# The token shift of the first projection: from TensorE matmuls with a shift matrix to DMA copies inside SBUF

## The chip, the cores and the metric

The kernel runs on one core of a Trainium2 chip. The metric is the device time of one execution in microseconds (us). Three executions of the kernel before took 3198.28, 3200.54 and 3200.67 us, so the median is 3200.54 us. A profiled execution, from which every row below is taken, took 3198.18 us.

## The reference, cut to what matters

The whole computation is two transformer-like blocks over 256 tokens of width 2048. The change touches one place, near the start: the input projection of the first block, and the token shift that follows it.

```
u   = x @ w_in                       # 256 x 2048 times 2048 x ...; the first 3360 columns are z
z_prev[0]  = 0
z_prev[t]  = z[t-1]                  # the row of the token before
z   = z + mu * (z_prev - z)          # mu: one value for each of the 3360 columns
r, k, v, zw, za, zg = split(z)       # feeds the rwkv stage: tanh, sigmoid, three small projections, the scan
```

The other columns of `u` (mlstm and gates) are not shifted. They are projected later in the kernel.

## The kernel before, in words

**Layout.** Tokens lie on the 128 partitions in two halves b = 0 and 1, so `UR` is [128 partitions, 2 halves, 3360 columns]: token 128*b + p is row p of half b. The row of the token before is thus one partition up, and for row 0 of half 1 it is row 127 of half 0.

**Stage "in".** The 3360 columns are done in seven chunks, ci = 0 to 6: six of 512 columns and one of 288. For each chunk TensorE multiplies `xT` by eight pieces of `w_in` (`pieces_a`, lines 590 to 620); a piece is 256 rows of the weight by the width of the chunk. All products are done in two halves of precision: a piece gives 12 matmuls (2 halves of tokens, 2 blocks of rows, 3 products of high and low parts), so a chunk has 96. The sum of a chunk is in a PSUM buffer; ScalarE copies it into `UR` (`out_of`, line 2709, event `ur.copied`). TensorE then waits for that copy and multiplies the chunk by two constant matrices, `shiftd` (one above the diagonal, minus one on it) and `carry` (the one row that passes from half 0 to half 1), lines 1282 to 1287: three plain fp32 matmuls over the width of the chunk, which the trace shows as six. They give z_prev - z in PSUM. VectorE multiplies that by mu in place and adds it to `UR` (lines 2246 to 2248, event `ur`). `mub`, the broadcast of mu, lies at `fmbase`.

**The weight pieces.** One stream of pieces serves the whole projection. SyncE loads a piece into one of six raw buffers as soon as the piece six places earlier has been halved (`pieces`, line 2962). ScalarE writes its high part, and VectorE (or GpSimd, for pieces that are marked so) subtracts to get the low part (`split_to`, line 207). There are three pairs of high and low buffers, so piece i can be halved only when TensorE has used piece i - 3. Every engine runs its own program in order; a call `split_to(j)` in an engine's program says at which point it does the pieces before j, and `ahead_of(key)` does those up to two beyond the last piece of that sum. Pieces 0 to 55 are those of the seven chunks, eight each, halved by VectorE. The pieces of the projection `ml.qk`, which follow, are halved by GpSimd.

**PSUM.** Four buffers of 1024 columns (`Ring`, `take`, line 116). TensorE takes the one that was taken longest ago, and waits until whoever reads it has freed it. The shift took a buffer of its own for each chunk.

**Order of the stages around it.** After chunk 6 and its shift, TensorE does three pieces of `ml.qk` (`rwkv`, line 691), then waits for `ur.gates`: tanh and sigmoid by ScalarE on the last columns of the shifted z (line 2375). It transposes them (`rw.lo`), does two more pieces of `ml.qk`, and then needs `ur.loraT`, which VectorE makes (lines 1402 to 1415) behind two products and two sums over the shifted k. GpSimd's program (line 2795) makes constants, issues eight loads for parameters, and then begins to halve the `ml.qk` pieces (`g.ahead_of("ml.qk", 1)`, line 2845).

Of the kernel before, what the change touches and what calls it, by code (L numbers as in the profile page):

```python
# [9 lines left out]
ALU = mybir.AluOpType  # L10
# [328 lines left out]
def build(nc, I, out, plan=None, last=False):  # L339
    with ExitStack() as ctx:  # L340
# [7 lines left out]
        def at(o, n, dt=F32):  # L348
            names[0] += 1
            assert o + n <= TOT, o + n  # L350
            return nc.alloc_sbuf_tensor_at(f"t{names[0]}", [128, n], dt, offset=base + 4 * o)[:, :]

        def alloc(n, dt=F32):
            o = top[0]
            top[0] = o + n + -n % 8
            return at(o, n, dt)

        def tm(c):
            return alloc(2 * c).rearrange("p (b c) -> p b c", b=2)
# [7 lines left out]
        def bufs(nraw, nhalf):  # L367
# [6 lines left out]
        ring = Ring(psum, plan.get("ring", {}))  # L374


        ident, shiftd, carry, ucent, tri_inc, tri_str = [alloc(128) for _ in range(6)]
        invm_at = top[0]
        invm = alloc(7 * 128)
        level = invm[:, 0:384].rearrange("p (l t) -> p l t", l=6)  # L380
# [8 lines left out]
        xT = [blocks[:, :, h, :] for h in range(2)]  # L389
# [3 lines left out]
        UR = tm(3360)  # L393
# [5 lines left out]
        fmbase = top[0]  # L399
# [9 lines left out]
        lt_at = top[0]  # L409
# [5 lines left out]
        kstate = alloc(8 * 64).rearrange("p (i v) -> p i v", i=8)  # L415
        pz = alloc(8)
        mub = at(fmbase, 3360)
        par = [RB.rearrange("p b c -> p (b c)")[:, 0:1024], RB.rearrange("p b c -> p (b c)")[:, 1024:2048],
               at(lt_at + 1280, 1024)]
        r_, k_, v_ = [UR[:, :, 1024 * i:1024 * i + 1024] for i in range(3)]  # L420
# [24 lines left out]
        sm2 = alloc(8 * 16).rearrange("p (k b h) -> p k b h", k=8, b=2)  # L445
        bg = alloc(32)
        gains = [at(invm_at + 768 + 16 * k, 16) for k in range(2)]
        diag = [shiftd, carry]
        assert top[0] <= invm_at + 896
        R = [rw[0:8, k, :] for k in range(8)]  # L450
        vhm = vm.rearrange("p b (h n) -> p b h n", n=128)
# [112 lines left out]
        def two(v, n):  # L564
            return v.unsqueeze(1).broadcast_to([128, 2, n])

        def half(v):
            return v.rearrange("p (b n) -> p b n", b=2)
# [5 lines left out]
        def tensor_program(e):  # L574
            pe = Tensor(e, counts, ring, stream, ident)

            def turn_columns(key, src, j, *after, of=(0, 1, 2, 3)):

                v = pe.take(key, j, of=of).rearrange("p (b k t) -> p b k t", b=2, k=4)
                pe.wait_ge(*after)  # L580
                for b in range(2):
                    for k in range(4):
                        pe.tr(v[:, b, k, :], src[:, b, 512 * j + 128 * k:512 * j + 128 * k + 128],
                              event=(key, j) if b == 1 and k == 3 else None)
# [62 lines left out]
            def proj_a(*args, **kw):  # L647
                for _ in pieces_a(*args, **kw):
                    pass
# [5 lines left out]
            def some(work, n):  # L655
                for _ in range(n):
                    next(work, None)
# [614 lines left out]
            for j, part in enumerate(((0,), (0, 1), (1, 2), (2, 3, 3))):  # L1272
                turn_columns("in.xT", x, j, (f"landed.in{j}",), ("ident",))
                for i in part:
                    pe.wait_ge(("in.xTc", i))
                    some(first, 1)
            pe.wait_ge(("consts",))
            for ci, c in enumerate(range(0, 3360, 512)):
                n = min(512, 3360 - c)
                if ci:  # L1280
                    proj_a(pe, f"ur{ci}", xT, 16, "w_in", c, n)
                v = half(pe.take("ur.shift", ci))[:, :, 0:n]
                d = UR[:, :, 512 * ci:512 * ci + n]
                pe.wait_ge(("ur.copied", ci))
                pe.mm(v[:, 0, :], shiftd, d[:, 0, :], True, True)
                pe.mm(v[:, 1, :], shiftd, d[:, 1, :], True, False)
                pe.mm(v[:, 1, :], carry, d[:, 0, :], False, True, event=("ur.shift", ci))
            pe.stage("rwkv")
            rwkv()
            rows_of("ml.if", "w_if", xT, (0, 8), 8, "pool")  # L1290
# [10 lines left out]
            v = pe.take("pl.T", of=(2,)).rearrange("p (k b t) -> p k b t", k=4, b=2)  # L1301
# [51 lines left out]
        def vector_program(e):  # L1353
            v = Vector(e, counts, ring, stream)
# [878 lines left out]
                    attended(u)  # L2233

            v.stage("in")
            v.stage("in")
            for j in range(4):
                v.split_to(2 * j + 1 if j else 0)
                low_half("in.xT", xT, j, "in.xTc")
                v.split_to(2 * j + 2)  # L2240
            for ci, c in enumerate(range(0, 3360, 512)):
                n = min(512, 3360 - c)
                v.ahead_of("ur.shift", ci)
                ps = half(v.bank("ur.shift", ci))[:, :, 0:n]
                d = UR[:, :, 512 * ci:512 * ci + n]
                v.wait_ge(("ur.shift", ci), ("landed.mu",))
                v.tt(ps, ps, two(mub[:, 512 * ci:512 * ci + n], n), ALU.mult)
                v.tt(d, d, ps, ALU.add, event=("ur", ci))
                v.free("ur.shift", ci)
            v.stage("rwkv")  # L2250
            rwkv()
            gate_rows()
# [13 lines left out]
            for c in range(4):  # L2266
# [8 lines left out]
                     event=("mi.lo", c))  # L2275
# [63 lines left out]
            for ci in range(4):  # L2339
                cs = slice(512 * ci, 512 * ci + 512)  # L2340
                for b in range(2):
                    v.stt(hn[:, b, cs], x[:, b, cs], inv[:, b:b + 1], rwt[:, cs], ALU.mult, ALU.mult,
                          event=("out.h", ci) if b else None)
# [451 lines left out]
        def pool_program(e):  # L2795
            g = Pool(e, counts, ring, stream)
# [2 lines left out]
            g.memset(ones, 1.0)  # L2799
            g.memset(ident, 0.0)  # L2800
            g.asel(ident, ident, ALU.not_equal, 1.0, 0, [[-1, 128]], 1, event=("ident",))
            g.memset(shiftd, 0.0)
            g.asel(shiftd, shiftd, ALU.not_equal, 1.0, 1, [[-1, 128]], 1)
            g.asel(shiftd, shiftd, ALU.not_equal, -1.0, 0, [[-1, 128]], 1)
            g.memset(carry, 0.0)
            g.asel(carry, carry, ALU.not_equal, 1.0, -127, [[128, 128]], 1)
            g.asel(tri_inc, one, ALU.is_ge, 0.0, 0, [[1, 128]], -1)
            g.asel(tri_str, one, ALU.is_gt, 0.0, 0, [[1, 128]], -1)
            g.memset(ucent, -CD)
# [4 lines left out]
            for l in range(6):  # L2814
                b = 1 << l
# [20 lines left out]
            def along(name):  # L2836
                return I[name][0].partition_broadcast(128)
# [3 lines left out]
                                    (gb[0:8, 1:2], I["f_bias"].rearrange("o h -> h o")), (bg, I["b_gate"])])  # L2841
            g.load(("landed.par",), [(par[0], along("k_k")), (par[1], along("k_a")),
                                     (par[2], I["r_k"][0].rearrange("h n -> (h n)").partition_broadcast(128))])
            g.stage("rwkv")
            g.ahead_of("ml.qk", 1)
            for b in range(2):
# [65 lines left out]
            for l in range(5):  # L2912
                n = 1 << l
# [6 lines left out]
            for l in range(3):  # L2920
                n = 1 << l
# [99 lines left out]
        with nc.Block() as block:  # L3021
            @block.sync
            def _(e):
                sync_program(e)

            @block.tensor
            def _(e):
                tensor_program(e)

            @block.vector  # L3030
            def _(e):
                vector_program(e)

            @block.scalar
            def _(e):
                scalar_program(e)

            @block.gpsimd
            def _(e):
                pool_program(e)  # L3040
# [55 lines left out]
```

## Time and profile before

| what | value |
|---|---|
| median of three executions | 3200.54 us |
| the profiled execution's own time | 3198.18 us |
| its span, from first to last instruction | 3196.4 us |
| TensorE busy | 3009.0 us, 94% of the span |
| VectorE busy | 1547.4 us, 48% |
| ScalarE busy | 837.8 us, 26% |
| GpSimd busy | 283.5 us, 9% |
| HBM read | 720.28 MB, 226 GB/s over the span |

In the trace PE is TensorE, DVE is VectorE, ACT is ScalarE, POOL is GpSimd and SP is SyncE; a q behind a name is that engine's sequencer. Code lines are those of the helpers (L137 matmul, L254 activation, L283 tensor_tensor of VectorE, L328 tensor_tensor of GpSimd, L83 a load), so instructions of a stage are found by time. Stage "in" with its shift runs from the start to about 192 us.

### The profile page before, as it was taken

What the parts mean: (1) busy time and instruction counts of PE and PEld (TensorE: products, weight loads), DVE (VectorE), ACT (ScalarE), POOL (GpSimd) and SP (SyncE); (2) the same over time, 40 slices, a digit from 0 to 9 for tenths busy, and PEclk for the clock granted to TensorE, in tenths of its full rate; (3) what the DMA queues carried; (4) which work ended last, traced back from release to release, by engine and by line L of the source; (5) the groups of instructions that cost most, each with busy time, mean ns of one, the idle gap of its engine ahead of it and who ended that gap; (6) DMA issues with size and microseconds to landing.
All of it is one profiled execution on the core that took longest, in us unless ns stands there. A gap on an engine that the chain in (4) does not pass through costs nothing.

```text
span 3196.4 us, 42548 instructions
## 1 busy us (share of the span) xinstructions
PE 3009.0 (94%) x18244; PEld 2161.4 (68%) x18244; DVE 1547.4 (48%) x1846; ACT 837.8 (26%) x926; POOL 283.5 (9%) x260
## 2 busy tenths in 40 slices
PE   8999999899999999999999999879999998999898
PEld 6777777899977743333333333268858878998886
DVE  4465544674556522222222222357887554444765
ACT  3352221544434310110110110010000243444443
POOL 2042111000000000000000000035440000000100
PEclk9999988999998999999999999989999999999999
DMA  7543221446575599999999999843333355898543
GB/s 244 151 139 100 74 61 58 123 140 182 174 237 171 190 366 425 425 425 425 425 425 425 425 425 425 341 159 118 114 124 118 126 178 125 194 194 183 137 165 138
DMA packets 216144, 725.25 MB, mean 227 GB/s; under 512 B 16314, under 2 KB 18794, under 8 KB 165644
## 3 DMA queue, kind: packets, MB, share of 16 engines
q1 hardware_dynamic: 210716, 702.22, 62.6%
q0 software_dynamic: 4144, 18.14, 1.6%
q8 instruction: 145, 2.38, 0.3%
q10 hardware_dynamic: 1088, 2.10, 0.2%
q14 instruction: 51, 0.42, 0.0%
HBM read 720.28 MB, written 2.11 MB: 226 GB/s over the span
## 4 chain that ended last, share of the span: by engine, by line
PE 72%; DMA 12%; DVE 11%; ACT 4%; issue 1%; POOL 0%; DVEq 0%; ACTq 0%
PE psum L137 71%; DMA t<-in_w_up 12%; DVE t L283 8%; ACT t L254 2%; PE psum L143 2%; DVE t L294 1%; ACT t L256 1%; DVE t L298 1%; DVE t L306 0%; ACT L254 0%; POOL t L328 0%; DVE t L269 0%; ACT L256 0%; DMA t<-in_x 0%; DVE t L275 0%
## 5 line engine op out<-in xcount | busy, mean ns | idle before, releaser
L137 PE MATMUL psum<-t,t 128*128 128x256 f32 (+7 forms) x17166 | 2914.8, 379 | 135.3 <-DVE t L283 78.8
L137 PEld LDWEIGHTS psum<-t,t 128*128 128x128 f32 (+4 forms) x17166 | 2069.7, 175 | 941.2 <-issue 564.2
L283 DVE TENSOR_TENSOR t<-t,t 128x1024 fp32r<-128x1024 f32 (+6 forms) x642 | 786.0, 1224 | 495.8 <-ACT t L254 462.5
L254 ACT ACTIVATE t<-t 128x1024 fp32r<-128x1024 f32 (+8 forms) x521 | 528.6, 1015 | 901.4 <-PE psum L137 625.3
L283 DVE TENSOR_TENSOR t<-t,psum 128x1024 f32<-128x1024 f32 (+3 forms) x265 | 246.3, 929 | 741.3 <-PE psum L137 440.7
L254 ACT ACTIVATE t<-psum 128x1024 f32<-128x1024 f32 (+5 forms) x278 | 213.5, 768 | 1414.9 <-PE psum L137 1315.5
L328 POOL TENSOR_TENSOR t<-t,t 128x1024 f32<-128x1024 f32 (+8 forms) x133 | 222.9, 1676 | 571.7 <-DVE t L283 258.2
L283 DVE TENSOR_TENSOR t<-psum,t 128x1024 f32<-128x1024 f32 (+6 forms) x117 | 101.1, 864 | 121.9 <-PE psum L137 91.8
L143 PE MATMUL psum<-t,t 128*128 128x128 f32 (+1 forms) x566 | 87.9, 294 | 31.7 <-DVE t L294 18.0
L143 PEld LDWEIGHTS psum<-t,t 128*128 128x128 f32 (+1 forms) x566 | 67.6, 150 | 69.5 <-issue 39.8
L83 POOL DMA_DIRECT2D t<-in_s_lr x1 | 0.6, 574 | 1187.2 <-DVE t L306 1187.2
L269 DVE COPY t<-psum 128x256 f32<-128x256 f32 (+4 forms) x74 | 44.4, 600 | 106.4 <-PE psum L143 59.7
L294 DVE SCALAR_TENSOR_TENSOR t<-t,t,t 128x512 f32<-128x512 f32 (+4 forms) x80 | 49.4, 618 | 3.0
L254 ACT ACT_TABLE_LOAD x38 | 48.8, 1283 | 4.6 <-issue 1.4
L298 DVE TENSOR_REDUCE t<-t 128x4 f32<-128x512 f32 (+9 forms) x58 | 47.5, 819 | 2.4 <-ACT t L254 0.4
L302 DVE TENSOR_TENSOR_SCAN t<-t,t 128x256 f32<-128x256 f32 (+1 forms) x65 | 44.7, 688 | 2.2
L137 PE MATMUL psum<-t 64*64 64x64 f32 (+2 forms) x512 | 36.3, 269 | 6.6 <-ACT t L254 5.8
L290 DVE TENSOR_SCALAR t<-t,t,t 128x64 f32<-128x64 f32 x128 | 40.2, 314 | 4.6
L137 PEld LDWEIGHTS psum<-t 64*64 64x64 f32 (+2 forms) x512 | 30.1, 174 | 10.1 <-ACT t L254 7.5
L83 POOL DMA_DIRECT2D f_rows<-t x1 | 0.6, 555 | 383.7 <-DVE t L302 383.7
L269 DVE COPY t<-t 64x64 f32<-64x64 f32 x64 | 30.2, 472 | 2.2
L256 ACT ACTIVATE t<-psum,t 128x256 f32<-128x256 f32 (+1 forms) x56 | 24.8, 444 | 21.5 <-PE psum L137 15.1
(67 smaller groups left out, 240.1 us busy)
## 6 DMA issues: line engine op xcount, KB each, us to landing
t<-in_w_gate SPq DMA_DIRECT2D x128, 1024.0 KB, 16.9
t<-in_w_up SPq DMA_DIRECT2D x128, 1024.0 KB, 18.4
t<-in_w_down SPq DMA_DIRECT2D x128, 1024.0 KB, 17.5
t<-in_w_in SPq DMA_DIRECT2D x160, 512.0 KB, 4.1
t<-in_w_in_odd SPq DMA_DIRECT2D x128, 512.0 KB, 5.4
t<-in_w_in_even SPq DMA_DIRECT2D x96, 512.0 KB, 3.8
t<-in_w_out SPq DMA_DIRECT2D x32, 512.0 KB, 4.3
t<-in_w_pg SPq DMA_DIRECT2D x32, 512.0 KB, 4.3
```

Of the source, the lines that this page charges most:

```text
L83: self.e.dma_start(out, in_).then_inc(self.counts.sem(name), 16)
L137: ins = self.e.matmul(o, l, r, start=start, stop=stop, skip_group_check=True)
L143: ins = self.e.transpose(o, i, self.ident[0:k, 0:k])
L254: self.put(self.e.activation(o, i, f, scale=scale), event)
L256: self.put(self.e.activation(o, i, f, bias=bias, scale=scale), event)
L269: self.put(self.e.tensor_copy(o, i), event)
L283: self.put(self.e.tensor_tensor(o, a, b, op), event)
L290: self.put(self.e.tensor_scalar(o, a, s1, s2, o1, o2), event)
L294: self.put(self.e.scalar_tensor_tensor(out=o, in0=a, scalar=s, in1=b, op0=o1, op1=o2), event)
L298: self.put(self.e.tensor_reduce(o, i, AX.X, op), event)
L302: self.put(self.e.tensor_tensor_scan(o, d0, d1, init, o0, o1), event)
L328: self.put(self.e.tensor_tensor(o, a, b, op), event)
```

## The change

The shift matmuls, their PSUM buffers and the two constant matrices go. In their place GpSimd waits for ScalarE's copy of a chunk and issues three DMA copies inside SBUF, which bring `UR` one partition down into a buffer `earlier[ci % 2]`: rows 0 to 111, rows 112 to 126, and the one row that goes from half 0 to half 1. VectorE then does three operations on SBUF (subtract, multiply by mu, add) instead of two. Row 0 of half 0 of the buffer is kept at zero by a memset. VectorE halves the pieces before 8*ci + 12, four pieces into the next chunk, before it waits for the copies of chunk ci. TensorE goes from chunk to chunk without the shift.

```diff
-        ident, shiftd, carry, ucent, tri_inc, tri_str = [alloc(128) for _ in range(6)]
+        ident, diag0, diag1, ucent, tri_inc, tri_str = [alloc(128) for _ in range(6)]
...
+        earlier = [at(o, 1024).rearrange("p (b c) -> p b c", b=2) for o in (fmbase + 3360, lt_at + 2304)]
...
# TensorE
+            for ci in range(1, 7):
+                proj_a(pe, f"ur{ci}", xT, 16, "w_in", 512 * ci, min(512, 3360 - 512 * ci))
             pe.wait_ge(("consts",))
-            for ci, c in enumerate(range(0, 3360, 512)):
-                n = min(512, 3360 - c)
-                if ci:
-                    proj_a(pe, f"ur{ci}", xT, 16, "w_in", c, n)
-                v = half(pe.take("ur.shift", ci))[:, :, 0:n]
-                d = UR[:, :, 512 * ci:512 * ci + n]
-                pe.wait_ge(("ur.copied", ci))
-                pe.mm(v[:, 0, :], shiftd, d[:, 0, :], True, True)
-                pe.mm(v[:, 1, :], shiftd, d[:, 1, :], True, False)
-                pe.mm(v[:, 1, :], carry, d[:, 0, :], False, True, event=("ur.shift", ci))
...
# VectorE
+            for z in earlier:
+                v.mset(z[0:1, 0, :], 0.0, event=("ur.first",))
...
             for ci, c in enumerate(range(0, 3360, 512)):
                 n = min(512, 3360 - c)
-                v.ahead_of("ur.shift", ci)
-                ps = half(v.bank("ur.shift", ci))[:, :, 0:n]
-                d = UR[:, :, 512 * ci:512 * ci + n]
-                v.wait_ge(("ur.shift", ci), ("landed.mu",))
-                v.tt(ps, ps, two(mub[:, 512 * ci:512 * ci + n], n), ALU.mult)
-                v.tt(d, d, ps, ALU.add, event=("ur", ci))
-                v.free("ur.shift", ci)
+                v.split_to(8 * ci + 12)
+                d, z = UR[:, :, c:c + n], earlier[ci % 2][:, :, 0:n]
+                v.wait_ge((f"landed.shift{ci % 2}", ci), ("landed.mu",))
+                v.tt(z, z, d, ALU.subtract)
+                v.tt(z, z, two(mub[:, c:c + n], n), ALU.mult)
+                v.tt(d, d, z, ALU.add, event=("ur", ci))
+                v.mset(z[0:1, 0, :], 0.0)
...
# GpSimd
-            g.memset(shiftd, 0.0)
-            g.asel(shiftd, shiftd, ALU.not_equal, 1.0, 1, [[-1, 128]], 1)
-            g.asel(shiftd, shiftd, ALU.not_equal, -1.0, 0, [[-1, 128]], 1)
-            g.memset(carry, 0.0)
-            g.asel(carry, carry, ALU.not_equal, 1.0, -127, [[128, 128]], 1)
...
+            for ci, c in enumerate(range(0, 3360, 512)):
+                n = min(512, 3360 - c)
+                d, z = UR[:, :, c:c + n], earlier[ci % 2][:, :, 0:n]
+                g.wait_ge(("ur.copied", ci), ("ur", ci - 2) if ci > 1 else ("ur.first",))
+                g.load((f"landed.shift{ci % 2}", ci), [(z[1:113], d[0:112]), (z[113:128], d[112:127]), (z[0:1, 1], d[127:128, 0])])
             g.stage("rwkv")
             g.ahead_of("ml.qk", 1)
```

## Rows read from the trace of the kernel before

**Rows 1.** The page: TensorE's busy time, and the chain that ended last by engine.
```profile
PE 3009.0 (94%) x18244; PEld 2161.4 (68%) x18244; DVE 1547.4 (48%) x1846; ACT 837.8 (26%) x926; POOL 283.5 (9%) x260
...
PE 72%; DMA 12%; DVE 11%; ACT 4%; issue 1%; POOL 0%; DVEq 0%; ACTq 0%
```

**Rows 2.** The chain of waits in order of time: start us, us, what.
```profile
38.88 1.03 ACT t L254
...
40.05 25.12 PE psum L137 x102
65.20 1.03 ACT t L254
...
171.49 2.86 PE psum L137 x6
...
187.67 0.66 ACT t L254
...
199.24 1.06 PE psum L143 x8
200.30 25.70 PE psum L137 x164
```

**Rows 3.** TensorE's timeline: start, us, instruction, count, [idle before <- releaser].
```profile
177.77 9.86 PE L137 MATMUL psum<-t,t 128*128 128x288 f32 x72 [0.25 <-DVE t L283]
188.37 10.36 PE L137 MATMUL psum<-t,t 128*128 128x288 f32 x78 [0.74 <-ACT t L254]
```

**Rows 4.** VectorE's timeline, same columns.
```profile
45.49 2.58 DVE L283 TENSOR_TENSOR t<-t,t 128x1024 fp32r<-128x1024 f32 x2
...
183.64 0.76 DVE L283 TENSOR_TENSOR t<-t,t 128x576 fp32r<-128x576 f32 x1 [0.84 <-ACT t L254]
...
191.79 3.53 DVE L283 TENSOR_TENSOR t<-t,t 128x2048 f32<-128x2048 f32 x1
...
204.09 0.48 DVE L279 MEMSET t<- 1x512 f32 x1 [0.16 <-DVE t L269]
...
228.13 1.23 DVE L294 SCALAR_TENSOR_TENSOR psum<-t,psum 128x1024 f32<-128x1024 f32 x1 [10.34 <-ACT t L254]
```

**Rows 5.** ScalarE's timeline around the last chunk, same columns.
```profile
195.94 1.46 ACT L254 ACTIVATE t<-t 128x1024 fp32r<-128x1024 f32 x2 [1.82 <-PE psum L137]
...
198.72 0.47 ACT L254 ACTIVATE t<-t 128x320 f32<-128x320 f32 x1
```

**Rows 6.** GpSimd's timeline, same columns.
```profile
26.39 0.54 POOL L83 DMA_DIRECT2D t<-in_r_k  x1
185.67 2.39 POOL L328 TENSOR_TENSOR t<-t,t 128x1024 fp32r<-128x1024 f32 x1 [158.74 <-ACT t L254]
...
194.20 3.38 POOL L328 TENSOR_TENSOR t<-t,t 128x1024 fp32r<-128x1024 f32 x1 [1.02 <-ACT t L254]
197.74 4.22 POOL L328 TENSOR_TENSOR t<-t,t 128x1024 fp32r<-128x1024 f32 x1 [0.17 <-POOL t L328]
```

**Rows 7.** DMA issues: out<-in, queue, count, KB each, us to landing; last row: all f_rows transfers.
```profile
t<-f_rows POOLq DMA_DIRECT2D x4, 512.0 KB, 5.7
...
t<-in_lnx_w POOLq DMA_DIRECT2D x4, 256.0 KB, 3.4
...
t<-in_mh_w POOLq DMA_DIRECT2D x1, 512.0 KB, 4.1
...
DMA to landing us min/median/max: 4.7/5.9/7.8
```

**Rows 8.** TensorE's timeline: two starts behind longer idle times.
```profile
236.24 29.59 PE L137 MATMUL psum<-t,t 128*128 128x256 f32 x168 [2.78 <-POOL t L328]
...
352.36 1.38 PE L137 MATMUL psum<-t,t 64*64 64x64 f32 x32 [2.40 <-DVE t L283]
```

**Rows 9.** Windows: span, busy PE, PEld, DVE, ACT, POOL, granted clock, DMA share, GB/s.
```profile
40.00:188.00 148.00, 141.77 (x612) 109.61 (x612) 67.34 (x58) 53.30 (x54) 2.33 (x1) 1.00 0.50 154
236.00:248.00 12.00, 11.76 (x75) 11.76 (x76) 11.83 (x6) 1.33 (x3) 8.94 (x4) 0.72 0.44 133
352.00:364.00 12.00, 10.99 (x140) 9.05 (x140) 4.73 (x6) 1.93 (x4) 2.32 (x3) 0.72 0.42 129
```

More of the change, by code:

```diff
@@ L447, in build @@
         gains = [at(invm_at + 768 + 16 * k, 16) for k in range(2)]
-        diag = [shiftd, carry]
+        diag = [diag0, diag1]
         assert top[0] <= invm_at + 896
@@ L2235, in vector_program @@
             v.stage("in")
-            v.stage("in")
+            for z in earlier:
+                v.mset(z[0:1, 0, :], 0.0, event=("ur.first",))
             for j in range(4):
```

## The prediction

> **What bounds the kernel now.** I read the page first: TensorE is busy for 94% of the span and is 72% of the chain that ended last [rows 1]. The question is therefore what TensorE does in the first 200 us, and the chain of waits in order of time answers it [rows 2]: TensorE for some 25 us, ScalarE's copy of 1.03 us, TensorE again, and so through the chunks. Nothing else is on it: VectorE is busy for 67.34 of the 148 us from 40 to 188, the DMA engines half of that, and the granted clock is 1.00 [rows 9]. TensorE's own work minus what it waits for sets the pace.
>
> **Sizes.** The three shift matmuls of a 512 chunk take 2.86 us [rows 2]. A stretch of 25.12 us has 96 matmuls of the next chunk beside them, so a chunk takes 25.12 - 2.86 = 22.26 and a piece 2.78 us. A piece of 288 columns takes 9.86/6 = 1.6 [rows 3].
>
> **What is removed.** Shifts 0 to 5: 6 x 2.86 = 17.2. The wait for ScalarE's copy ahead of a shift: from 65.17, where the stretch that starts at 40.05 ends, to 66.27, where the one after the copy at 65.20 starts, 1.1 us, in chunks 1 to 5: 5.5. Chunk 0 keeps its wait: without buffers for shifts the ring gives chunk 1 the buffer of chunk 0, which the copy has yet to free. The 0.25 idle at 177.77 [rows 3] goes. Behind chunk 6: the wait of 0.74 and a shift of 288/512 x 2.86 = 1.6. Sum: 17.2 + 5.5 + 0.2 + 2.3 = 25.2 us. That is the whole possible gain, and the rest is what comes back.
>
> **When the shifted rows are there.** T is the end of a chunk's matmuls. The copy ends at T + 1.1, and GpSimd starts to issue at T + 1.2. An issue takes 0.54 [rows 6], so three take 1.65; the large copy goes first. Its landing is the unknown: no copy inside SBUF is in this trace. It moves 448 KB in rows of 2 KB. The nearest rows are GpSimd's load of 512 KB, 4.1 us from issue to landing, and of 256 KB, 3.4; loads of the same queue from `f_rows` took 4.7 to 7.8 [rows 7]. One load of weights at least runs beside it. Ends: 3.4 and 7.8. I take 4.6, nearest to the 4.1 with half a microsecond for that traffic; the small copies, issued 0.5 and 1.1 later, should be there by then. Landing at L = T + 5.8.
>
> The Trainium skill (DMA: Bandwidth & Descriptors, Anatomy of one DMA, SWDGE path) gives 2.0 us plus bytes over 436 GB/s for a DMA that GpSimd issues; as an estimate that is 3.05 us here, and the gain below would be some 3 us larger. The 4.1 us that the trace has for 512 KB is above that rule's 3.2, so the rows decide.
>
> **Who waits for it: VectorE, with the weight pieces behind it.** After the landing VectorE does three operations of 1.29 (2.58/2) and a memset of 0.48 with its gap, 0.6 together [rows 4], and only then the low part of the piece four places into the next chunk, 1.23: ready at L + 5.75 = T + 11.55. TensorE wants it at T + 4 x 2.78 = T + 11.1. So 0.4 us of idle in each of the chunks 2 to 5, 1.7 in all (chunk 1 starts 1.2 later and is covered). At a landing of 3.4 it is nothing; at 7.8 it is 3.6 each. The piece before that one costs nothing: its low part is ready at T + 5.1, wanted at T + 8.3.
>
> **Chunk 6 has no such cover.** Its pieces take 1.6, so TensorE wants the fifth at T + 6.4. VectorE has it at L + 3.87 + 0.6 + 0.78 (low part of 576 columns, 0.76 [rows 4]) = T + 11.05. Idle: 4.6 us (2.2 with the landing at 3.4, 7.8 with it at 7.8).
>
> **GpSimd is behind its issues too.** Before, its first `ml.qk` low part began at 185.67 [rows 6], ahead of the end of chunk 6. Now it stands behind the wait for the copy of chunk 6: copy at T + 0.7, three issues to T + 2.5, 2.39 for the low part, T + 4.9. TensorE has nothing else to do: idle 4.9 us. Then come the pieces at 2.4 against TensorE's 2.8, but GpSimd's low parts took 3.38 and 4.22 while VectorE ran its 2048-column product [rows 4, 6]; the fifth piece then comes 0.7 late. Sum behind chunk 6: 5.6. If GpSimd's queue costs nothing there, 0.7; no reason for a gain.
>
> Ready for the last columns: landing at T + 4.5, three short operations to T + 6.9; ScalarE needs its two pieces first and then tanh, a table and sigmoid [rows 5], as now, so this wait is as before. VectorE's work from there to `loraT` is 204.57 - 191.79 = 12.8 [rows 4], T + 20; TensorE wants it at about T + 21. VectorE's idle of 10.34 before 228.13 [rows 4] takes up its later start after that. Where the 25.70 us of TensorE at 200.30 starts is what counts [rows 2], and all behind it moves with it.
>
> **The clock.** Now there is no idle over 1.2 us between 40 and 188, and the clock stays at the higher of its two levels, 2.4 GHz. Behind an idle time of 2.78 and one of 2.40 [rows 8] the twelve microseconds had a mean of 0.72 [rows 9], between full and half (1.2 GHz): 0.28 x 12 = 3.4 us lost. The two new idle times of 4.6 and 4.9 would cost up to 6.8. They stand close together, and in both a slower TensorE partly uses time in which the next low part is not ready. I take 3.5; ends 0 and 6.8.
>
> **Other edits.** Two memsets and three selects of GpSimd go at the start, where nothing waits for its loads; VectorE's first two memsets are ahead of its first operation; VectorE's third operation per chunk lies in its free half. Nothing each.
>
> **Sum.** 25.2 - 1.7 - 4.6 - 5.6 - 3.5 = 9.8 us. The profiled execution took 3198.18 (span 3196.4 and 1.8 around it), which gives 3188.4; it lay 2.4 below the median of the runs, so I forecast 3190.7 us.
>
> **Rivals.**
> 1. *Quick landing, steady clock.* Landing 3.6, no idle in chunks 2 to 5, 3.7 in chunk 6, 5.6 behind, no clock loss: 25.2 - 9.3 = 15.9, 3184.7 us. For it: the load of 256 KB at 3.4. Against it: two idle times over 2.4 with no clock loss would be new. Chance 0.22.
> 2. *Late landing, slower than before.* The copies of 15 rows or one row, or SBUF as source, bring the landing to 7.8, the far end of the rows. Then 4 x 3.6 = 14.4 in chunks 2 to 5, 7.8 in chunk 6, 5.6 + 2.5 behind it (VectorE now late with `loraT`), and a clock that falls in every chunk, 3.5 + 8: 25.2 - 41.8 = 16.6 slower, 3217 us. It decides from about 6.3 us from issue to landing. For it: f_rows. Against it: that source is HBM just written and its rows are shorter. Chance 0.13.
> 3. *In between, no change to be measured.* Landings of 5.5 to 6.3, or full clock losses, gain of 0 to 6: about 3197. At the 5.7 of the f_rows median [rows 7]: idle 1.5 x 4 + 5.7 + 5.6 + 3.5 = 20.9, gain 4.3. Chance 0.20.
>
> The forecast, gains of 6.4 to 13, has 0.45. About 0.2%, 6.4 us, is what a measurement can tell from no change. Faster 0.67, same 0.20, slower 0.13. The range 3182 to 3203 holds case 1 but its edge, case 3 whole, and the start of case 2.
>
> **What would show it.** After a 512 chunk TensorE runs on with no idle (but for 1.2 after chunk 0), and a chunk takes 22.3 us. VectorE idles at about T + 5.1 to T + 5.8, released by the DMA. TensorE idles once inside chunk 6, released by VectorE, and once after it, released by GpSimd L328. The clock is under 1.00 from 170 on. The chunks end at about 165 instead of 187.65, plus the idle of chunk 6. The prediction is wrong if the copies land after 6 us, if TensorE waits in every chunk, or if the lead at `rw.lo` is lost later in the rwkv stage.

## The result and the profile after

The changed kernel is slightly slower than the one before: 20 runs of each had medians of 3201.86 us (3195.9 to 3209.31) and 3197.2 us (3190.48 to 3202.13); the ratio is 1.0016 with a 95% interval of 1.001 to 1.0022, some 5 us. The forecast was 10 us less. That 3201.86 lies inside the forecast range of 3182 to 3203 is luck: the range was set from a median of 3200.54 for the kernel before, which came out at 3197.2 over 20 runs, and by the ratio the changed kernel would have stood at 3205.7 on the old one. The profiled execution after took 3209.31 us (span 3207.6). It is the slowest of the twenty, 11.2 us of span over the profiled one before, so its rows show the causes in a strong form; about half of what it lost is not in the medians.

TensorE's work is less, as the diff says; it is the idle time and the clock that took it back. TensorE's timeline after has the same columns as [rows 3]:

```profile
39.49 11.41 PE L137 MATMUL psum<-t,t 128*128 128x512 f32 x48 [1.11 <-ACT t L254]
51.41 22.66 PE L137 MATMUL psum<-t,t 128*128 128x512 f32 x96 [0.51 <-DVE t L283]
76.62 23.89 PE L137 MATMUL psum<-t,t 128*128 128x512 f32 x96 [2.55 <-DVE t L283]
102.58 24.13 PE L137 MATMUL psum<-t,t 128*128 128x512 f32 x96 [2.08 <-DVE t L283]
127.58 22.56 PE L137 MATMUL psum<-t,t 128*128 128x512 f32 x96 [0.87 <-DVE t L283]
151.86 17.86 PE L137 MATMUL psum<-t,t 128*128 128x512 f32 x96 [1.72 <-DVE t L283]
175.73 9.40 PE L137 MATMUL psum<-t,t 128*128 128x288 f32 x48 [6.01 <-DVE t L283]
190.38 11.10 PE L137 MATMUL psum<-t,t 128*128 128x256 f32 x72 [5.24 <-POOL t L328]
202.11 1.03 PE L143 MATMUL psum<-t,t 128*64 128x128 f32 x8 [0.63 <-ACT t L254]
202.90 5.94 PE L137 MATMUL psum<-t,t 128*128 128x256 f32 x48
210.91 30.97 PE L137 MATMUL psum<-t,t 65*128 65x512 f32 x168 [2.07 <-DVE t L279]
```

Each stretch that VectorE releases begins four pieces into a chunk, where the forecast put the wait: five of 0.51 to 2.55 us in chunks 1 to 5 (7.7 in all), 6.01 in chunk 6, then 5.24 released by GpSimd. The chunks end at 175.73 + 9.40 = 185.1 us, 2.5 before the 187.65 of the kernel before, where 22.9 were counted as removed.

The chain of waits has taken the copy in; columns as in [rows 2]. One turn of it, from the end of chunk 2 to the middle of chunk 3:

```profile
89.39 1.03 ACT t L254
...
90.70 0.98 POOL t L83 x2
...
91.95 4.81 DMA t<-t
96.78 1.24 DVE t L283
98.04 1.24 DVE t L283
99.30 1.24 DVE t L283
...
100.69 0.49 DVE t L279
...
101.30 1.24 DVE t L283
...
102.58 12.99 PE psum L137 x48
```

ScalarE's copy, GpSimd's issues, the DMA, VectorE's three operations and memset, then the low part of a weight piece, and only then TensorE. The "x2" says which copy the chain goes through: the last of three. The DMA issues give each of them, from its own issue to its landing (columns as in [rows 7]):

```profile
t<-t POOLq DMA_DIRECT2D x6, 448.0 KB, 3.7
...
t<-t POOLq DMA_DIRECT2D x6, 60.0 KB, 3.5
...
t<-t POOLq DMA_DIRECT2D x6, 2.0 KB, 4.4
```

The large copy is faster than I took it for (3.7 against 4.6). The 2 KB copy, issued 1.2 us later, takes longer than it. From the first issue the last row is there after 1.2 + 4.4 = 5.6 in the medians (6.06 in the turn above, from 90.70 to 96.76).

VectorE and GpSimd around chunk 6 answer to [rows 4] and [rows 6]. First VectorE:

```profile
189.40 7.14 DVE L283 TENSOR_TENSOR t<-t,t 128x576 f32<-128x576 f32 x3 [8.86 <-DMA t<-t]
...
197.06 4.49 DVE L283 TENSOR_TENSOR t<-t,t 128x2048 f32<-128x2048 f32 x1
...
210.28 0.48 DVE L279 MEMSET t<- 1x512 f32 x1 [0.17 <-DVE t L269]
...
236.56 1.23 DVE L294 SCALAR_TENSOR_TENSOR psum<-t,psum 128x1024 f32<-128x1024 f32 x1 [12.39 <-ACT t L254]
```

and GpSimd:

```profile
186.11 1.75 POOL L83 DMA_DIRECT2D t<-t  x3 [19.68 <-ACT t L254]
187.88 5.20 POOL L328 TENSOR_TENSOR t<-t,t 128x1024 fp32r<-128x1024 f32 x2
193.25 2.67 POOL L328 TENSOR_TENSOR t<-t,t 128x1024 fp32r<-128x1024 f32 x1 [0.17 <-POOL t L328]
```

Three operations of 576 elements take 7.14 us while GpSimd subtracts; the low parts of 576 elements took 0.76 each before, with GpSimd idle [rows 4]. I use the last row of VectorE as a mark below, the **decay mark**: its first operation behind the decay exponentials, at 228.13 before [rows 4] and at 236.56 here, 8.4 later. The stretch from the end of chunk 6 to the mark thus grew from 40.5 to 51.4 us.

The granted clock, columns as in [rows 9], of the chunks after, and of the stretch behind chunk 6 after:

```profile
40.00:185.00 145.00, 131.26 (x575) 107.21 (x574) 77.60 (x70) 52.54 (x53) 10.36 (x18) 0.94 0.59 177
185.00:235.00 50.00, 42.06 (x248) 35.23 (x247) 33.46 (x18) 20.98 (x22) 32.77 (x14) 0.86 0.38 120
```

and of the kernel before from chunk 6 to the exponentials:

```profile
188.00:226.00 38.00, 37.12 (x251) 31.78 (x252) 26.72 (x16) 20.11 (x21) 30.04 (x11) 1.00 0.47 150
```

Between the two levels of 2.4 and 1.2 GHz, the clock was never down there before and is down for parts of both stretches now.

### The profile page after: what moved, and what is told of

The parts are those of the page before. It is cut to its first block, busy times and chain, and to the rows that moved or that the text cites. A ratio compares the mean times of both kernels' runs of the same rounds, so it can differ in the third digit from the quotient of the medians.

```text
span 3207.6 us, 42503 instructions
## 1 busy us (share of the span) xinstructions
PE 3003.5 (94%) x18202; PEld 2162.8 (67%) x18202; DVE 1567.8 (49%) x1862; ACT 837.7 (26%) x926; POOL 289.4 (9%) x276
## 4 chain that ended last, share of the span: by engine, by line
PE 70%; DVE 13%; DMA 12%; ACT 4%; issue 1%; POOL 0%; DVEq 0%; ACTq 0%
PE psum L137 68%; DMA t<-in_w_up 11%; DVE t L283 10%; ACT t L254 2%; PE psum L143 1%; DVE t L294 1%; DVE t L298 1%; ACT t L256 1%; DMA t<-t 1%; DVE t L306 0%; DVE t L269 0%; POOL t L83 0%; ACT L256 0%; ACT L254 0%; POOL t L328 0%
## 5 line engine op out<-in xcount | busy, mean ns | idle before, releaser
L137 PE MATMUL psum<-t,t 128*128 128x256 f32 (+8 forms) x17124 | 2908.6, 380 | 151.5 <-DVE t L283 93.8
L137 PEld LDWEIGHTS psum<-t,t 128*128 128x128 f32 (+5 forms) x17124 | 2070.6, 176 | 950.6 <-issue 563.3
L283 DVE TENSOR_TENSOR t<-t,t 128x1024 fp32r<-128x1024 f32 (+7 forms) x663 | 815.6, 1230 | 517.9 <-ACT t L254 463.1
L283 DVE TENSOR_TENSOR t<-t,psum 128x1024 f32<-128x1024 f32 (+3 forms) x258 | 238.3, 924 | 742.6 <-PE psum L137 441.9
```

The lines of the kernel that those rows point to most:

```text
L137: ins = self.e.matmul(o, l, r, start=start, stop=stop, skip_group_check=True)
L283: self.put(self.e.tensor_tensor(o, a, b, op), event)
```

## The experiments

Ratios are to the kernel before, each with its 95% interval.

**1. VectorE waits later (`late16`).**

```diff
-                v.split_to(8 * ci + 12)
+                v.split_to(8 * ci + 16)
```

> The changed kernel, but VectorE halves all eight pieces of the next chunk before it waits for the copies of a chunk (8*ci + 16 in place of 8*ci + 12). Theory A (the lead is eaten by VectorE waiting for the copies with weight pieces behind it): TensorE has no idle time in chunks 2 to 6, the chunks end near 165.5 us instead of 185.2, the clock stays 1.00 until there. What is lost behind chunk 6 (10.9 us against the kernel before, counted from the end of chunk 6 to the first decay exponential) stays, so the time is some 11 us below the kernel before, ratio 0.9965. Rival B (traffic inside SBUF slows the weight loads or the matmuls): idle times and stretched chunks stay though nothing waits behind the copies. Rival C (the rwkv stage ends at the same time whatever the start): the chunks end early but the ratio to the kernel before stays at 1.00.

Measured: 3186.03 us, ratio 0.9965 (0.9952 to 0.9979). TensorE's timeline:

```profile
39.84 125.68 PE L137 MATMUL psum<-t,t 128*128 128x512 f32 x576 [1.11 <-ACT t L254]
170.77 11.07 PE L137 MATMUL psum<-t,t 128*128 128x256 f32 x72 [5.25 <-POOL t L328]
```

One stretch of 576 matmuls, with no idle time and the clock at 1.00 (window below), ends at 165.5. Against it the changed kernel's same 576 took from 39.49 to 185.13, 145.6 us: 13.7 of idle (the six rows released by VectorE) and 131.9 of matmuls, 6.2 over 125.68, which is the clock. Three things follow. The traffic inside SBUF slows nothing that can be seen here (rival B falls). The lead is not lost later (rival C falls). And VectorE's wait with weight pieces behind it, with the clock that fell behind it, cost 5 + 11 = 16 us by the ratios. The end at 165.5 is 22.1 us ahead of the kernel before, so of the 22.9 counted as removed all but 0.8 came. The copies themselves take longer here, and nothing waits for them (the window first, then the issues):

```profile
40.00:165.00 125.00, 125.00 (x574) 102.31 (x575) 75.99 (x69) 52.83 (x53) 10.65 (x18) 1.00 0.69 202
```
```profile
t<-t POOLq DMA_DIRECT2D x6, 448.0 KB, 6.0
...
t<-t POOLq DMA_DIRECT2D x6, 2.0 KB, 6.4
```

**2. And chunk 6 by TensorE (`late16_mm6`).** Chunks 0 to 5 as in 1; the two constant matrices are back.

```diff
...
+                if ci >= 6:
+                    v = half(pe.take("ur.shift", ci))[:, :, 0:n]
+                    d = UR[:, :, 512 * ci:512 * ci + n]
+                    pe.wait_ge(("ur.copied", ci))
+                    pe.mm(v[:, 0, :], diag0, d[:, 0, :], True, True)
+                    pe.mm(v[:, 1, :], diag0, d[:, 1, :], True, False)
+                    pe.mm(v[:, 1, :], diag1, d[:, 0, :], False, True, event=("ur.shift", ci))
...
```

The rest of the edit makes the constants on GpSimd, gives VectorE its two old operations for chunk 6, and takes away GpSimd's copies for it.

> As late16, and chunk 6 alone is shifted by TensorE with the two constant matrices, as in the kernel before, so GpSimd issues nothing behind chunk 5. Theory A: the chunks end near 165.5 and all behind it takes as long as in the kernel before (38.4 us from the end of chunk 6 to the first decay exponential): 22 us below the kernel before, ratio 0.9931. Rival C: ratio 1.00. If GpSimd's queue and its contention with VectorE are not the cause of the loss behind chunk 6, it gains no more than late16.

Measured: 3177.38 us, ratio 0.9931 (0.9917 to 0.9944), the best of all: some 22 us under the kernel before. The decay mark is at 207.26, 20.9 earlier than before. VectorE, and then two rows of GpSimd from the same time:

```profile
161.76 8.81 DVE L283 TENSOR_TENSOR t<-t,t 128x576 fp32r<-128x576 f32 x4 [0.84 <-ACT t L254]
...
171.33 0.77 DVE L283 TENSOR_TENSOR psum<-psum,t 128x576 f32<-128x576 f32 x1
172.13 0.75 DVE L283 TENSOR_TENSOR t<-t,psum 128x576 f32<-128x576 f32 x1
172.99 2.29 DVE L283 TENSOR_TENSOR t<-t,t 128x2048 f32<-128x2048 f32 x1
...
207.26 1.23 DVE L294 SCALAR_TENSOR_TENSOR psum<-t,psum 128x1024 f32<-128x1024 f32 x1 [7.56 <-ACT t L254]
```
```profile
169.66 3.17 POOL L328 TENSOR_TENSOR t<-t,t 128x1024 fp32r<-128x1024 f32 x1 [0.17 <-POOL t L328]
173.00 4.51 POOL L328 TENSOR_TENSOR t<-t,t 128x1024 fp32r<-128x1024 f32 x1 [0.17 <-POOL t L328]
```

The two operations with an operand in PSUM keep their 0.77 and 0.75 though GpSimd subtracts then too. The first row is a low part and the three operations of chunk 5's shift, all with both inputs in SBUF: they now meet GpSimd, and the row takes 8.81 against 4.61 in kernel 1, but TensorE does not wait for it. Kernel 1 has its mark at 216.81; the 9.6 between them is what it costs to shift chunk 6 by copies and not by TensorE.

**3. Chunk 6 by TensorE alone (`mm6`)**, with the wait at 8*ci + 12 left as it is; the rest of the edit is that of 2.

> The changed kernel with its wait at 8*ci + 12 as it is, but chunk 6 alone shifted by TensorE. Theory A: everything up to the end of chunk 6 stays as in the changed kernel (13.7 us idle, slow clock, end near 185), and the part behind it takes the 38.4 us of the kernel before and not 49.3: 2 to 3 us faster than the kernel before, ratio 0.999, and 8 to 10 us faster than the changed kernel. If the loss behind chunk 6 comes from the clock that fell inside chunk 6 and not from GpSimd's queue, the idle time behind chunk 6 goes but the matmuls stay slow and the ratio stays at 1.001.

Measured: 3193.03 us, ratio 0.999 (0.998 to 1.0001), 8 us less than the changed kernel by the ratios. Its profile shows the chunk stretches of 22.6 us with idle times of 0.35, 1.53, 1.01, 1.45 and 0.80 and no loss of clock, and 5.82 in chunk 6 with one:

```profile
170.67 8.97 PE L137 MATMUL psum<-t,t 128*128 128x288 f32 x48 [5.82 <-DVE t L283]
```

These 48 matmuls took 6.6 at full clock before (9.86/72 x 48 [rows 3]). From the end of chunk 6 at 179.64 to the mark at 220.28 it takes 40.6 us, as in the kernel before (40.5): the whole loss behind chunk 6 is gone. One part of the expectation missed. Up to the end of chunk 6 this kernel waits as the changed one does, but that end came at 179.6 and not near 185, for 5.1 us idle in chunks 1 to 5 and not 7.7, with no clock lost there. The changed kernel's profiled execution is thus an unfavourable one in its chunks. What copies do behind chunk 6 and the waits in the chunks are two separate losses, 8 and 16 us by the ratios, 24 together; kernel 2 against the changed one is 27, within the intervals.

**4. GpSimd one piece ahead (`late16_pool57`).** Kernel 1, and:

```diff
+                if ci == 6:
+                    g.split_to(57)
                 g.wait_ge(("ur.copied", ci), ("ur", ci - 2) if ci > 1 else ("ur.first",))
```

> The kernel with the wait at 8*ci + 16, in which GpSimd makes the first low part of ml.qk (piece 56) before it waits for the copy of chunk 6. Theory A3: the idle time of 5.25 us behind chunk 6 falls to about 2 (piece 57 still stands behind the issues), with less clock loss; the copies of chunk 6 are issued a few tenths later. Gain over 8*ci + 16 alone: 3 to 5 us, ratio 0.9953 to the kernel before. If TensorE's idle time there only moves into the next waits (ur.gates, ur.loraT), the gain is under 1 us.

Measured: 3180.63 us, ratio 0.9955 (0.9942 to 0.9969), some 3 us less than kernel 1; the intervals overlap, so the gain is not shown. The idle time released by GpSimd fell from 5.25 to 0.58 and 1.53, but TensorE then waits for ScalarE's gates:

```profile
165.54 3.09 PE L137 MATMUL psum<-t,t 128*128 128x256 f32 x24 [0.58 <-POOL t L328]
170.15 5.96 PE L137 MATMUL psum<-t,t 128*128 128x256 f32 x48 [1.53 <-POOL t L328]
181.42 1.89 PE L143 MATMUL psum<-t,t 128*64 128x128 f32 x8 [5.30 <-ACT t L254]
```

VectorE has the shifted columns at 179.15: its three slow operations start at 172.71, behind the landing. So the wait for the gates, which are made from them, is the next one. Both expectations hold in part.

**5. GpSimd held back (`late16_poolwait`).** Kernel 1, and:

```diff
             g.stage("rwkv")
+            g.wait_ge(("ur", 6))
             g.ahead_of("ml.qk", 1)
```

> A measurement, not a version: the wait at 8*ci + 16, and GpSimd makes no low part of ml.qk before VectorE has finished the shift of chunk 6. Theory A4 (VectorE's operations with both inputs in SBUF and GpSimd's subtractions slow each other): the three 576-element operations of chunk 6, 7.06 us together beside GpSimd, take 2.3 to 2.4 us with GpSimd idle, and start as before. Rival (they are slow because of the copies' own traffic in SBUF): they stay at 7. TensorE waits some 4 us longer behind chunk 6 either way.

Measured: VectorE's three operations with GpSimd idle, and its next one with GpSimd at work:

```profile
170.07 2.35 DVE L283 TENSOR_TENSOR t<-t,t 128x576 f32<-128x576 f32 x3 [3.39 <-DMA t<-t]
...
172.93 4.06 DVE L283 TENSOR_TENSOR t<-t,t 128x2048 f32<-128x2048 f32 x1
```

2.35 against 7.06 in kernel 1: GpSimd's subtractions are what slows VectorE, and the copies' traffic is not. The time, 3184.08 us, ratio 0.9965 (0.9954 to 0.9977), is that of kernel 1, not 4 us more: TensorE idles 9.57 behind chunk 6, but the wait for `loraT` (2.06 in kernel 1) is gone, and with it the slow clock behind that wait: the 168 matmuls that took 30.93 there take some 27.5 here (a stretch of 216 takes 33.40, and 48 of them 5.93 in kernel 1). That I had not expected, and it gives an estimate of what that wait costs TensorE: 2.06 + 3.4, some 5.5 us.

**6. The copy of 112 rows alone (`big_only`).**

```diff
-                v.mset(z[0:1, 0, :], 0.0, event=("ur.first",))
+                v.mset(z, 0.0, event=("ur.first",))
...
-                g.load((f"landed.shift{ci % 2}", ci), [(z[1:113], d[0:112]), (z[113:128], d[112:127]), (z[0:1, 1], d[127:128, 0])])
+                g.load((f"landed.shift{ci % 2}", ci), [(z[1:113], d[0:112])])
```

> A measurement that leaves out part of the shift: only the copy of 112 rows is made, the copies of 15 rows and of one row are left out, and those rows of the buffer are zero or old. Theory A1 (with three copies the last one lands 5.6 us after the first issue, and that is what broke the cover): landing at the end of a chunk + 5.0, idle in chunks 1 to 5 under 1.5 us in all instead of 7.7, in chunk 6 about 4, and with the clock some 8 to 12 us less than the changed kernel, ratio 0.998. Rival (the large copy itself, with VectorE's queue, sets it): within 3 us of the changed kernel.

Measured: 3192.89 us, ratio 0.9988 (0.9979 to 0.9997), by the ratios 9 us less than the changed kernel. The waits are 1.13, 1.61 and 0.38 in chunks 1 to 5 (3.1 in all), 4.50 in chunk 6, and 4.15 behind it. The two small copies, with their issues, therefore cost 9 us. Part of the expectation missed: the large copy took 4.5 here, not 3.7, so more waits remained. Why it is slower alone is open. But 4.5 is what the prediction had given it, so this kernel tests the rest of its sum: with that landing the idle is 3.1 and 4.5 us for the 1.7 and 4.6 forecast, and still the kernel gains 4 us and not 10.

**7. The single row first (`rowfirst`).**

```diff
-                g.load((f"landed.shift{ci % 2}", ci), [(z[1:113], d[0:112]), (z[113:128], d[112:127]), (z[0:1, 1], d[127:128, 0])])
+                g.load((f"landed.shift{ci % 2}", ci), [(z[0:1, 1], d[127:128, 0]), (z[113:128], d[112:127]), (z[1:113], d[0:112])])
```

> The changed kernel with the three copies of a chunk issued in the other order: the one row first, the 112 rows last. Theory A1 (the single-row copy, issued last and 4.4 us from issue to landing, is what VectorE waits for): if its 4.4 us is its own latency, it is hidden now, the large copy is issued 1.2 us later and lands 3.7 later, at about 6.2 us after the end of a chunk instead of 7.0; five idle times shrink by 0.8 each, some 4 to 6 us faster than the changed kernel with the clock. Rival: each copy queues behind the ones before it, so the last lands when all data has landed whatever the order: same time as the changed kernel, within 2 us.

Measured: 3206.83 us, ratio 1.0026 (1.0016 to 1.0036): not faster, if anything slower. The issues tell why:

```profile
t<-t POOLq DMA_DIRECT2D x6, 448.0 KB, 4.3
t<-t POOLq DMA_DIRECT2D x6, 60.0 KB, 2.8
...
t<-t POOLq DMA_DIRECT2D x6, 2.0 KB, 2.3
```

Issued first, the single row takes 2.3; its 4.4 was not its own. The last of the three lands 4.3 to 4.4 after its issue in both orders. The shifted rows were there 6.5 to 6.7 us after the ends of chunks 1 to 4, but 8.8 after that of chunk 5, and TensorE idles 7.73 in chunk 6 for it. My first theory, that the single row is slow in itself, is refuted; that the cost is the third issue and its place in the queue fits kernels 6 and 7, but no run separates the two.

**8. ScalarE issues the copies (`act_issue`)**, behind its own copy out of PSUM, with the same pairs; GpSimd's loop of copies goes.

```diff
+                a.ordered()
+                a.wait_ge(("ur", ci - 2) if ci > 1 else ("ur.first",))
+                a.load((f"landed.shift{ci % 2}", ci), [(z[1:113], d[0:112]), (z[113:128], d[112:127]), (z[0:1, 1], d[127:128, 0])])
```

> The changed kernel with the same three copies issued by ScalarE right behind its own copy out of PSUM, not by GpSimd. Theory A3 (GpSimd's queue): TensorE's idle time of 5.2 us behind chunk 6, released by GpSimd, falls under 1.5, for 4 to 8 us less than the changed kernel. If descriptors made by GpSimd's software are slow, the landing after the end of a chunk falls from 7.0 to under 6 us as well and another 5 us come back. Rival (the idle times only move the clock's drops about): under 2 us of difference. Against it: three issues of about half a microsecond are put ahead of ScalarE's high parts.

Measured: 3200.1 us, ratio 1.0006 (0.9997 to 1.0015), 3 us less than the changed kernel by the ratios, with intervals that overlap, and under the expectation. TensorE's idle time released by GpSimd behind chunk 6 is 0.57, as expected, and the copies of the 512-column chunks land 3.2 to 3.9 after issue. But the high parts of the weight pieces stand behind ScalarE's issues, three of which took 3.12 us from 89.79, and TensorE waits twice per chunk:

```profile
77.24 17.06 PE L137 MATMUL psum<-t,t 128*128 128x512 f32 x72 [1.77 <-DVE t L283]
95.34 5.84 PE L137 MATMUL psum<-t,t 128*128 128x512 f32 x24 [1.03 <-DVE t L283]
...
198.93 1.89 PE L143 MATMUL psum<-t,t 128*64 128x128 f32 x8 [5.85 <-ACT t L254]
```

## Why the prediction was wrong

The sum was 25.2 - 1.7 - 4.6 - 5.6 - 3.5. Two steps failed: the landing of the copies, with the small ones put at nothing, and what the clock loses for the idle times that follow from it. A third, VectorE's time behind chunk 6, was put at nothing. Term by term, in the profiled execution:

- **Removed, 25.2: right but for 0.8.** The shifts and their waits are gone; the one wait of chunk 0 stayed (1.11). Kernel 1 ends its chunks 22.1 us earlier, where 22.9 had been counted up to there.
- **The landing, T + 5.8: too early, and the step that failed first.** Landings came 7.5, 7.4, 6.2, 7.0 and 7.0 us after the ends of chunks 1 to 5. I had bounded the large copy well, and set the small ones aside with "should be there by then". They carry the landing (kernels 6 and 7). The idle was 7.7 in chunks 1 to 5 and 6.0 in chunk 6, for 1.7 and 4.6. The mechanism, its place and the piece that waits were as forecast; the size was not. It also gave TensorE a wait in every chunk, which the prediction had named as a sign of being wrong; chunk 1, which it held to be covered, waits 0.51. Issue to last landing was 5.6, in the case that I had priced as "in between, no change".
- **GpSimd behind its issues, 4.9: right** (5.24, and 0.57 where ScalarE issues). The 0.7 for the fifth piece did not come.
- **VectorE behind chunk 6: wrong.** I had three short operations to T + 6.9 and `loraT` at T + 20, in time. They end at T + 11.4, `loraT` is there at 210.8 = T + 25.6, and TensorE waits 2.07 for it. I had read GpSimd's subtractions as slowed by VectorE [rows 4, 6], and did not ask the reverse; nor that the change takes VectorE's operands out of PSUM. Kernel 5 shows the reverse, and kernel 2 that an operand in PSUM is spared.
- **The clock, 3.5: far too small.** In the chunks it was 6.2, as kernel 1 tells. Behind chunk 6, the 72 matmuls took 11.10 for 9.1 at full clock (kernel 8, 183.94 to 193.07), 2.0, and the stretch from `loraT` to the exponentials 23.5 (210.91 to 234.44) for 20.0 before (206.04 to 226.02), 3.5: 11.7 in all. I had counted two new idle times; there were five over 2 us. Behind the two that I had counted, 2.8 (9.40 for 6.6) and 2.0 were lost, 4.8 for my 3.5; the other 6.9 fell behind the three that I had not. In the medians the clock takes less: this execution is 7.4 above its median, and the profiled kernels 3 and 7, whose waits in chunks 1 to 5 were all under 1.8 us, lost none there.
- **Later stages** add or lose little: the mark is 8.4 late, the span 11.2. The other 2.8 I have not traced; single executions of one kernel differ by more than that.

Idle 6.0 + 1.4 + 0.3 - 0.7 + 2.1, clock 8.2, later 2.8: 20.1 of the 20.9 us between the forecast of -9.8 and this execution's +11.1; the rest is about what was not removed. In the medians, 15 us lie between forecast and result, and the two small copies account for 9 of them (kernel 6).

The slower rival had the right mechanism and a chance of 0.13, but needed a landing at 7.8. It came at 5.6 with the clock and the contention, and a slower kernel all the same. The point at which the case turned, 6.3 from issue to landing, was placed too far out because the terms for the clock and for VectorE were too small. One figure of the working is wrong in itself: with a landing at 3.4 the idle in chunk 6 would be 3.4 us (T + 4.6 + 5.25 against T + 6.4), not 2.2; the forecast does not use it.

## What to carry to other kernels

Before moving work off the bounding engine, list what stands *behind* the new wait in each queue that it enters, and put the wait where everything that the bounding engine needs next has been done: moving one constant from 12 to 16 turned 0.16% slower into 0.35% faster. Keep the old way for the last piece of a loop, which has no next piece to hide behind: that gave the other half, 0.69% in all. Price a group of DMAs to the landing of its last member (here 1.2 + 4.4 us), and not by its largest one. Price the clock for every new idle time as long as those that cost it in the rows below. And ask of each engine not only whom it waits for, but whom it slows where it runs.

## What the runs showed of the hardware

- VectorE with both inputs in SBUF and a GpSimd subtraction at the same time disturb each other. On short operations VectorE is slowed threefold, by experiment: 7.06 us for three of 576 elements against 2.35 with GpSimd idle. With one operand in PSUM: 0.77 and 0.75, undisturbed. The Trainium skill (SBUF — State Buffer, Who interferes with whom) says that tensor_tensor with both inputs in SBUF contends with GpSimd's reads; these runs agree.
- Either engine can be the one that loses. In kernel 2 VectorE's product of 2048 elements started at 172.99, 0.01 us ahead of GpSimd's subtraction, and took 2.29 while the subtraction took 4.51; in kernel 5 the product started 0.43 us behind a subtraction and took 4.06. GpSimd's subtraction took 2.39 where it ran undisturbed [rows 6].
- Copies inside SBUF of 448 KB took 3.7 us from issue to landing in the changed kernel, where the weight loads pause and keep 0.59 of the DMA engines busy, and 6.0 in kernel 1, where they run on at 0.69. That the loads are the reason is not tested; kernel 6, with no small copies behind the large one, had 4.5.
- The clock after an idle time: in these profiles none was lost behind idle times of up to 1.77 us; behind 2.55 and 2.08 the following 96 matmuls took 23.89 and 24.13 for 22.6; behind 4.50 to 7.73, four pieces of 288 columns took 8.8 to 9.4 for 6.6.
